# Expert stage of a diffusion block: the down weights are requested by ScalarE at the head of each block instead of by SyncE

## What is computed

```
def expert_block(args):
    xb, e = args                       # xb: 128 x 1024 rows, e: the block's expert
    hid = jax.nn.silu(xb @ lp["ex_w_gate"][e]) * (xb @ lp["ex_w_up"][e])    # 128 x 512
    return hid @ lp["ex_w_down"][e]                                         # 128 x 1024

y = lax.map(expert_block, (xin, block_e)).reshape(n_rows, D_MODEL)
```

## Time and profile before

| | us |
|---|---|
| median of 3 runs | 3189.16 |
| lowest, highest | 3187.28, 3192.15 |
| profiled execution, first to last instruction | 3182.9 |
| of it, steady part of the expert loop (window 2430 to 3060) | 630 |
| of that window: PE, ACT, DVE busy | 590.4, 531.7, 515.7 |
| one block, from one second cast of `hid` to the next (2610.82 to 2630.57) | 19.75 |

### The profile page before, as it was taken

The page is one execution under the profiler, slowest core; times in us unless marked ns, Lnnn a source line. Parts: engine busy times, 40 slices in busy tenths (PEclk is TensorE's granted clock), DMA queues, the critical chain, the costliest instruction groups (busy, mean ns, idle before and its releaser), DMA issues. The chain is left out here.

```text
span 3182.9 us, 33378 instructions
## 1 busy us (share of the span) xinstructions
PE 2769.4 (87%) x12400; PEld 2050.8 (64%) x12400; DVE 1631.1 (51%) x1517; ACT 996.2 (31%) x1104; POOL 279.9 (9%) x236
## 2 busy tenths in 40 slices
PE   7889898989999599999894999998918999999973
PEld 4443773335888577878773778784417888888861
DVE  4634336272332256343178262424627888888866
ACT  2302230001332133320000010001007888888860
POOL 1200000000000221000141300000010000000001
PEclk9889999999999788999996999998958999999996
DMA  6432454221232421211110111113149999999945
GB/s 213 132 126 112 166 205 135 89 86 60 67 108 84 135 78 52 71 53 51 40 51 14 47 34 47 43 30 121 50 189 366 371 375 374 371 371 371 373 183 224
DMA packets 92001, 482.89 MB, mean 152 GB/s; under 512 B 10836, under 2 KB 20324, under 8 KB 76745
## 3 DMA queue, kind: packets, MB, share of 16 engines
q1 hardware_dynamic: 71688, 382.41, 33.5%
q0 software_dynamic: 20224, 99.25, 8.3%
HBM read 424.01 MB, written 82.78 MB: 159 GB/s over the span
## 5 line engine op out<-in xcount | busy, mean ns | idle before, releaser
L337 PE MATMUL ps<-uT_upper_rest,ring_rest 128*128 128x512 f32 x1360 | 541.3, 398 | 0.0
L337 PEld LDWEIGHTS ps<-uT_upper_rest,ring_rest 128*128 128x128 f32 x1360 | 259.0, 190 | 66.1
L337 PE MATMUL ps<-uT_upper_rest,cs_upper 128*128 128x512 f32 x320 | 130.2, 407 | 55.0 <-DVE cs_val L1971 46.8
L2443 PE MATMUL ps<-ring_rest,uT_rest 128*128 128x256 f32 (+1 forms) x416 | 135.2, 325 | 26.2 <-DVE uT_upper_rest L2520 26.2
L2445 PE MATMUL ps<-ex_u_raw_rest,uT_rest 128*128 128x256 f32 x560 | 156.6, 280 | 0.0
L2443 PE MATMUL ps<-ex_upper,uT_rest 128*128 128x256 f32 (+1 forms) x424 | 136.3, 322 | 21.0 <-DVE uT_upper_rest L2520 21.0
L337 PE MATMUL ps<-uT_upper_rest,xbc_upper 128*128 128x512 f32 x336 | 136.0, 405 | 6.1 <-DVE ring_rest L727 6.1
L1744 PE MATMUL ps<-sb_merged,ring 128*128 x256 | 114.5, 610 | 26.0 <-DVE sb_merged L1819 26.0
L2444 PE MATMUL ps<-ex_upper,uT_rest 128*128 128x256 f32 (+1 forms) x424 | 134.3, 317 | 0.0
L337 PE MATMUL ps<-uT_rest,xbc_upper 128*128 128x512 f32 x336 | 134.2, 399 | 0.0
L2444 PE MATMUL ps<-ring_rest,uT_rest 128*128 128x256 f32 (+1 forms) x416 | 133.3, 320 | 0.0
(11 more groups left out here) (437 smaller groups left out, 6305.6 us busy)
## 6 DMA issues: line engine op xcount, KB each, us to landing
sb_spare<-in_ex_g SPq DMA_DIRECT2D x35, 2048.0 KB
ex_u_raw<-in_ex_u SPq DMA_DIRECT2D x35, 2048.0 KB
sb_merged<-in_ex_d SPq DMA_DIRECT2D x35, 2048.0 KB, 10.3
ring<-in_w_mod SPq DMA_DIRECT2D x48, 512.0 KB, 4.5
sb_uT<-moe SPq DMA_DIRECT2D x35, 512.0 KB, 12.0
moe<-sb_uT POOLq DMA_DIRECT2D x35, 512.0 KB, 8.0
ring<-in_w_gate SPq DMA_DIRECT2D x32, 512.0 KB, 3.6
ring<-in_dft SPq DMA_DIRECT2D x24, 512.0 KB, 3.6
```

What stands on the lines that cost most here:

```text
L337: last = self.nc.tensor.matmul(out, weight, x[:, k, lo:hi], start=(k == 0 and n == 0), stop=(k == kt - 1 and n == 2))
L2443: nc.tensor.matmul(out, left_up, w_up, start=first, stop=False)
```

## The change

SP's loop no longer requests down. ACT does, at the head of its own body: it reads the block's expert out of `plan`, waits on the same counter for the same value (`AHEAD - CH` is 10), and starts the transfer into the same buffer. The values that the casts wait for stay as they were.

```
@@ SP
                     e = sp.value_load(plan[0:1, bass.ds(i, 1)], min_val=0, max_val=EXPERTS - 1)
-                    for m, name in enumerate(("ex_g", "ex_u", "ex_d")):
+                    for m, name in enumerate(("ex_g", "ex_u")):
                         sp.wait_ge(used, i * CH + (AHEAD - 2 * CH + 2 * m + 2))
                         sp.dma_start(raw[m][:, b, :], item(a[name], e)).then_inc(w_in[m][b], 16)
                     sp.wait_ge(sent, 2 * TT * 16)
@@ ACT
                 def body(i, b, j):
+                    e = act.value_load(plan[0:1, bass.ds(i, 1)], min_val=0, max_val=EXPERTS - 1)
+                    act.wait_ge(used, i * CH + (AHEAD - CH))
+                    act.dma_start(raw[2][:, b, :], item(a["ex_d"], e)).then_inc(w_in[2][b], 16)
                     act.wait_ge(x_mm, i + 2)
```

## The result

The changed kernel takes 3263.15 us (median of 4, 3253.89 to 3268.12) against 3188.22 us of the kernel before (median of 4): ratio 1.0235, 95% interval 1.0214 to 1.0256. It is 75 us slower; 46 were forecast. The profiled execution has a span of 3263.7 us, 80.8 above the one before; single executions scatter by some us, so that the two profiled ones lie 81 us apart where the medians lie 75 apart.

The account below looks back on a forecast made before the run. The prediction took a ring through ACT, DVE and PE, 19.75 us per block, as the bound, not the transfers. 3189.2 + 46 (41 head, 5 late down) = 3235 us; forecast 3215 to 3255, whole range 3208 to 3280.

Parts of the forecast that it names:

- The ring: Cycle of ACT's block start, chunk 0 on ACT and DVE, PE's gate, up and turning of `hid`: 19.75 us per block.
- The head's size: Read, wait and DMA request added at ACT's block start: 1.2 us per block, 41 us over 34 blocks (24 to 54).
- That is just under the 10.7 that it has: Down's transfer: landing about 10.5 us after ACT's request, with 10.7 us until chunk 4 needs it.
- a wait of over 1 us ahead of chunk 4: Sign on ACT, before casting chunk 4, that would prove the assumed sharing between queues wrong.
- the sharing: ACT's down transfer and SP's queue on the DMA engines: pieces go in turn, so down lands in about 10.5 us.
- some 2.7 MB are moved by 8.8: SP's queue: of gate and up's 4.2 MB, this much moved 8.8 us after gate's request, leaving 1.5 MB beside down.
- down passes 1.5 MB of up and a little of the rows: Data moved during down's transfer: 2.1 + 1.5 + 0.1 MB at 0.38 MB per us, 9.7 us.
- the 0.15 put in: ACT's waits for late down at chunk 4: 0.15 us per block, 5 us in all; ends 0 and 1.5 us.
- A long wait checks itself: After a long wait for down at chunk 4, the later request meets less of up; no size given.
- The clock: Rival: PE's longer wait ahead of gate drops it to 1.2 GHz, 1.5 us or more per block, 3285 and up; chance 0.05.
- a down that lands late in most blocks: Rival: ACT waits 1 to 2 us at chunk 4 in most blocks, 3260 to 3300, centre 3275; chance 0.17.

Follow-up runs that it names:

- e2_head_warm: Kernel before plus ACT's new head with a 2 KB transfer, and 14 unused PE transposes at each block's head: 3216.59 against 3183.79 us, ratio 1.0095.
- e1_head: Kernel before, SP still requesting down early, plus ACT's new head with a 2 KB transfer instead of 2 MB: 3238.97 against 3183.79 us, ratio 1.0165.
- e4_early: Changed kernel with ACT's request of down moved behind chunk 5 of the block before: 3186.43 against 3183.79 us, ratio 1.0002.

## Why the prediction was right, and where it was short

**The ring: right.** Three runs bear it out: the head's 1.13 us lengthen a block from 19.72 to 20.85, chunk 0 taken off the ring shortens it to 18.24, and with chunk 0 gone the head costs 23 us instead of 55 (of which some 38 were the head itself, the rest slow stretches).

**The head's size: right.** 1.2 us were taken from SP's rows, 1.13 measured (36.3 / 32), 34 x 1.13 = 38 us forecast as 41; e2_head_warm has 33 by the medians and 34 x (20.84 - 19.72) = 38 by the periods. The alternation was seen too: 1.25 us where the loop jumps back, 1.02 elsewhere for the forecast 1.1.

**"That is just under the 10.7 that it has": the term that was mis-sized.** The time that down has was right: 10.8 us (2615.38 to 2626.17). The landing was not: 11.8 us (median; 9.5 to 13.2) for 10.5. By the prediction's own sign, a wait of over 1 us ahead of chunk 4, seen in 16 of 32 blocks, the sharing was wrong. The trace tells which step of it. Bytes of each queue (q1 is SP's, q10 ACT's; packets, MB, share of the 16 engines), from one request of gate (2628.23) through the 8.8 us of the prediction, then from there to the cast that waited for down (2648.16); ACT requests at 2636.01:

```profile
q1 hardware_dynamic: 181, 2.70, 88.6%
```
```profile
q10 hardware_dynamic: 144, 2.10, 44.0%
q1 hardware_dynamic: 250, 2.02, 43.2%
```

The step that failed is not "some 2.7 MB are moved by 8.8", which came out to the digit, but "down passes 1.5 MB of up and a little of the rows", 0.1 MB in the sum. SP's queue moved 2.02 MB beside down's 2.10, and 2.70 + 2.02 = 4.72 MB is all that it had: gate, up and the whole 0.5 MB of rows. In every block of the loop SP's queue had moved its 4.7 MB by the time down landed. The two queues shared in turn, as the prediction had it; but then 1.5 MB of up and 0.5 MB of rows, together less than down's 2.1, all pass before down ends. So 4.1 MB had to go where the sum had 3.7; at its own 0.38 MB per us and with its 0.8 us of start-up that makes 11.6 us. The end was slow as well, 117 GB/s in the last 2 us:

```profile
2625.38:2628.23 2.85, 2.85 (x15) 2.39 (x14) 2.85 (x2) 2.83 (x3) 0.53 (x1) 1.00 0.10 42
...
2646.01:2648.01 2.00, 2.00 (x6) 1.52 (x6) 2.00 (x2) 0.88 (x1) 0.47 (x1) 0.53 0.29 117
```

Before gate's request (first row) the DMA engines stand nearly idle, at 42 GB/s, time that they had used for down in the kernel before: requested early it fills a gap, requested late it makes one. The waits came to 0.83 us per block for the 0.15 put in. "A long wait checks itself" was right: after the longest wait, 2.42 us, the next request came 10.3 us after gate's instead of 7.8, and down landed in 9.5 us.

**The clock: a rival at 0.05 that came true.** It was costed as "1.5 us or more" for a stretch, and a stretch on the ring costs 1.6; but the chance came from one wait of 2.02 us after which the clock stayed. Repeated in every block, waits of 2.2 to 2.4 us brought a slow stretch in about one block of five (e1_head, 5 in 26 blocks of the window) and nearly every second (the changed kernel, 12 in 25, where PE's second wait comes on top). The case was written as all or nothing, where it is a share: 22 us with the head alone, 28 in the changed kernel (14 and 30 by the periods). The Trainium skill, in "TensorE: Matmul & The Clock Gate", section "Why this matters for your kernels", advises against idle gaps above about 3 us between bursts of products; by that rule the clock would have stayed, and here it fell with waits of 2.2 to 2.4 us.

Together: 33 (head) + 14 (down, with the clock held) + 28 (clock) = 75 us. This sum proves nothing by itself, since each term is the difference between one run and the next. What bears it out is the periods: 34 x (20.84 - 19.72) = 38 for the head, where its rows give 34 x 1.13 = 38; 13 for down, where the waits give 13; 30 for the clock; 81 in all, the difference of the two profiled spans. The parts are not independent: a slow stretch lengthens a block and gives down time to land, and a wait for down makes PE wait again. So 28 is what holding the clock gives back, not a price that stands alone.

**Where luck came in.** With the clock held, the change costs 47 us (51 by the periods), close to the 46 of the forecast. The clock's 28 were in neither the sum nor the range: its rival stood at 3285 and up. The result lies above the forecast's own 3215 to 3255, and fell inside the whole range because the upper end, 3280, had been drawn for a down that lands late in most blocks, at 41 us more; of that, some 8 came beyond the 5 put in, and the clock filled the room. That a slower kernel was forecast, and by which ring, is no luck; that 3263 lay inside the range is in part.

## What to carry to other kernels

Before an instruction goes to another engine, see whether its new place lies behind a wait on the ring of engines that sets the period. ACT's queue had no room to run ahead behind such a wait, so a read, a few registers and a DMA issue cost their full 1.1 us there, and nothing one wait earlier (e4_early). A transfer that has always been early may be what keeps the DMA engines busy in the gap: count what stands before and beside it at its new time, to the last byte of the other queues. And the same reading that priced the loss gave a gain of 57 us: what ends the wait of the busiest engine, and can that step be done in the idle time of another?

## What the hardware showed that I had not expected

- Repeated waits of PE of 2.2 to 2.4 us in a period of 20.9 us brought stretches at 1.2 GHz, in which a 128x512 product takes 0.63 us instead of 0.40. Filling 1.7 us of the wait with useless transposes kept the clock at 2.4 GHz and made the kernel with the head alone 14 to 22 us faster, the changed kernel 28 to 30.
- Down, requested by ACT when SP's queue still held 2.3 MB, landed only when all of these had been moved too: SP's queue moved 2.02 MB beside down's 2.10 in the last 11 us.
- A DMA share of 0.97 at 372 GB/s was no limit: at 403 GB/s and a share of 1.00 nobody waited for a transfer.
- An issue by ACT costs its queue 0.35 us (SP 0.34, POOL 0.53), and ACT's read of the table takes 0.28 us in the loop where the single one ahead of it took 0.46.
